# Router products on the scaled residual, with root and shift applied to the logits, in a one-core hybrid transformer layer

## The reference, cut to what matters

```python
def _layer(x, c, ...):
    mod = (silu(c) @ w_ada + b_ada)          # sh1, sc1, gt1, sh2, sc2, gt2 per sequence
    ...
    x = x + gt1 * mix                         # mix = merged @ w_out
    h = _rms_norm(x, norm_ffn_w) * (1 + sc2) + sh2
    x = x + gt2 * _hier_moe(h, lp)

def _hier_moe(h, lp):
    g_logits = t @ w_group_router + b_group_router      # 4 groups
    g_sel = argmax(g_logits)                            # and its softmax probability
    e_logits = t @ w_expert_router + b_expert_router    # 32 experts, 8 of the group kept
    top_p, top_i = top_k(softmax(e_logits), 2)
    comb = p_group * top_p / sum(top_p)
    out = sum over the 2 experts of comb * (silu(t@gate) * (t@up)) @ down
```

## Time and profile before

| | us |
|---|---|
| median of 3 runs | 838.47 |
| lowest, highest | 837.27, 840.47 |
| the profiled execution, its own time | 839.85 |
| its span in the trace | 838.1 |
| TensorE busy | 728.8 (87%) |
| weight loads busy | 529.4 (63%) |
| VectorE, ScalarE, POOL busy | 264.0, 195.1, 97.5 |
| mean granted TensorE clock, of full | 0.942 |

### The profile page before, as it was taken

How to read it: one execution, slowest core, us unless ns; L and a number is a source line. 1 busy time by engine, 2 the same in 40 slices (tenths; PEclk the granted TensorE clock), 3 DMA queues, 4 the chain that set the end, 5 groups by cost and what they waited for, 6 DMA issues and landing times.

```text
span 838.1 us, 19950 instructions
## 1 busy us (share of the span) xinstructions
PE 728.8 (87%) x8393; PEld 529.4 (63%) x8394; DVE 264.0 (32%) x737; ACT 195.1 (23%) x500; POOL 97.5 (12%) x229
## 2 busy tenths in 40 slices
PE   2779999999988975998988999973998989999985
PEld 1567777787766654776766777733655656656554
DVE  0145412430134350666683112144111111111122
ACT  1221113112731322122223200051111112121225
POOL 7000000001011222100000000001212221222200
PEclk9869999999999996999998999985899999999996
DMA  7835579999444954651002706875899999999901
GB/s 264 228 103 201 201 245 327 327 327 334 121 112 122 260 148 103 200 179 26 1 2 74 266 0 268 334 300 204 313 413 411 414 413 411 415 412 414 385 15 56
DMA packets 108728, 195.88 MB, mean 234 GB/s; under 512 B 9964, under 2 KB 71097, under 8 KB 100488
## 3 DMA queue, kind: packets, MB, share of 16 engines
q1 hardware_dynamic: 106760, 189.94, 63.1%
q0 software_dynamic: 1920, 5.25, 1.7%
HBM read 185.40 MB, written 9.77 MB: 233 GB/s over the span
## 4 chain that ended last, share of the span: by engine, by line
PE 81%; DVE 6%; DMA 4%; issue 4%; ACT 3%; SPq 1%; POOL 0%; ACTq 0%; DVEq 0%; POOLq 0%
PE ps L1142 17%; PE ps L533 10%; PE ps L1212 7%; PE ps L506 5%; PE ps L546 5%; PE ps L430 4%; PE ps L451 4%; PE ps L1084 4%; PE ps L509 3%; PE ps L434 2%; PE ps L496 2%; DMA arena<-in_w_ada 1%; SPq L811 1%; PE ps L540 1%; DVE arena L1894 1%
## 5 line engine op out<-in xcount | busy, mean ns | idle before, releaser
L1142 PE MATMUL ps<-arena 128*128 128x288 f32 x576 | 144.8, 411 | 0.0
L1142 PEld LDWEIGHTS ps<-arena 128*128 128x128 f32 x576 | 109.3, 192 | 31.2 <-issue 1.0
L533 PE MATMUL ps<-arena 128*32 128x128 f32 x2432 | 86.7, 278 | 15.3 <-issue 12.8
L533 PEld LDWEIGHTS ps<-arena 128*32 128x32 f32 x2432 | 69.3, 111 | 39.4 <-issue 38.2
L1212 PE MATMUL ps<-arena 128*128 128x288 f32 x256 | 76.2, 427 | 14.2 <-DMA arena<-in_w_in 10.3
L1212 PEld LDWEIGHTS ps<-arena 128*128 128x128 f32 x256 | 45.3, 194 | 30.1 <-DMA arena<-in_w_in 10.6
L506 PE MATMUL ps<-level,arena 32*128 32x256 f32 x624 | 44.8, 401 | 0.5 <-DVE arena L775 0.5
L546 PE MATMUL ps<-arena,hact 128*32 128x256 f32 x608 | 40.7, 385 | 0.0
L770 DVE TENSOR_TENSOR h_row<-h_row,ps 128x64 f32<-128x64 f32 x38 | 8.4, 221 | 96.6 <-ACT h_row L628 96.6
L404 POOL DMA_INDIRECT arena<-h_rows,idx_now x38 | 37.6, 988 | 9.5 <-issue 9.5
L1084 PE MATMUL ps<-arena,cT 128*32 128x128 f32 x1024 | 33.8, 292 | 4.6 <-DMA arena<-in_w_ada 4.6
(11 more groups left out here) (432 smaller groups left out, 983.0 us busy)
## 6 DMA issues: line engine op xcount, KB each, us to landing
arena<-in_w_exp_gate SPq DMA_DIRECT2D x32, 1024.0 KB
arena<-in_w_exp_up SPq DMA_DIRECT2D x32, 1024.0 KB
arena<-in_w_exp_down SPq DMA_DIRECT2D x32, 1024.0 KB
arena<-in_w_ada SPq DMA_DIRECT2D x12, 2048.0 KB, 10.2
arena<-in_w_in SPq DMA_DIRECT2D x18, 1024.0 KB, 5.9
arena<-in_w_ada_final SPq DMA_DIRECT2D x4, 2048.0 KB, 14.9
arena<-in_w_in SPq DMA_DIRECT2D x16, 512.0 KB, 4.7
arena<-in_state_ssm_rec SPq DMA_DIRECT2D x8, 512.0 KB, 6.0
```

Source lines behind the costliest of these rows:

```text
L533: l = mm(ps[CW * q:CW * (q + 1), 5, 0:P].rearrange("p (g f) -> p g f", g=2), xwin[:, at:at + CW], gate_up[:, :, k, f:f + HF], start=(k == ...
L1142: l = mm(ps[:, 2 + 2 * sl + m, 0:TOK], w_ring[sl][:, k, m * P:(m + 1) * P], HN[:, k, :], start=(k == 0), stop=(k == KT - 1))
```

## The change

The router's 8 products move into the output projection. ScalarE copies each prompt tile of xT times the scale into H2 right after squaring it (squares go to a buffer of their own, `sq2`), VectorE does the samples; TensorE then does tile k's router product behind its mean-square product (`logits`). The shift's part of the logits, shift @ w_rt, is 8 small products ahead of the projection (9 sequences by 36), to which VectorE adds the bias (`b_seq`). When the root is there, VectorE multiplies the 36 rows of logits by it, and TensorE transposes them and adds `seq_row` times `b_seq` (6 small products). The norm of H2 itself (times root, plus shift) is done by POOL in 8 + 1 instructions and by ScalarE in 8, beside the routing. The combining weights (`r_m`) are computed after the indices, and the second 24 slot products wait for them. In the loop the samples' part of PT is a block matrix of 128 columns, and one product takes the place of four. Place 6 of the ring loads its down weights first, and gate and up after the tables are done with.

```diff
+        q = ex_at + 2 * EXW + 3 * D
         r_n, q = carve(q, 4, E)
         r_c, q = carve(q, E)
         r_w, q = carve(q, 2, 6)
-        GE, q = carve(q, 6, NWIN + 1)
...
-        A6, q = carve(q, 6, NWIN)
+        GE, _ = carve(q, 6, NWIN + 1)
+        r_q, q = carve(q, E, 8)
+        A6, q = carve(q + 62, 6, NWIN)
...
-        PT, iota = late[:, 0:TOK], late[:, TOK:2 * TOK]
...
+        PTW = SEQ + 4 * SMP
+        PT, iota = late[:, 0:PTW], late[:, PTW:2 * PTW]
...
             wgu, wd = ex[6]
+            load(wd, wd_[:, 6], "ex_ld6")
+            e.wait_ge(S("count_mm"), 3)
+            e.wait_ge(S("tab"), 1)
             load(wgu[:, 0:KT, :], wg_[:, 6], "ex_ld6")
             load(wgu[:, KT:2 * KT, :], wu_[:, 6], "ex_ld6")
-            e.wait_ge(S("count_mm"), 3)
-            e.wait_ge(S("tab"), 1)
-            load(wd, wd_[:, 6], "ex_ld6")
...
-            e.wait_ge(S("x2"), KT)
-            link(g.iota(iota, pattern=[[1, TOK]], base=0, channel_multiplier=0, allow_small_or_imprecise_dtypes=True))
+            e.wait_ge(S("gate_mm"), NGATE)
+            e.wait_ge(S("merged"), KT)
+            link(g.memset(seq_row, 1.0))
...
+            g.memset(lg_row[:, TOK:], 0.0).then_inc(S("iota"), 1)
...
             e.wait_ge(S("stored"), 16 * rec_stores[0])
             g.memset(y_row, 0.0).then_inc(S("y_row"), 1)
             g.memset(PT, 0.0).then_inc(S("pt"), 1)
+            e.wait_ge(S("root"), 2)
+            e.wait_ge(S("rt_mm"), 2)
+            for k in range(KT):
+                g.tensor_tensor(out=H2[:, k, :], in0=H2[:, k, :], in1=rstd[:], op=ALU.mult).then_inc(S("h2"), 1)
+            e.wait_ge(S("h2"), KT)
+            s = H2[:, :, SEQ:TOK].rearrange("p k (b t) -> p k b t", t=NT)
+            g.tensor_tensor(out=s, in0=s, in1=modT[:, SHIFT2:SHIFT2 + KT, 1:NC].unsqueeze(3).broadcast_to([P, KT, NB, NT]),
+                            op=ALU.add).then_inc(S("h2"), 1)
...
-                l = mm(ps[:, bank, 0:TOK], ones[:, :], (H2 if n == 2 else sq3)[:, k, :], start=(k == 0), stop=(k == KT - 1))
+                l = mm(ps[:, bank, 0:TOK], ones[:, :], (sq2 if n == 2 else sq3)[:, k, :], start=(k == 0), stop=(k == KT - 1))
...
+
+            for k in range(KT):
+                l = mm(ps[0:NC, 2, 0:EG + E], modT[:, SHIFT2 + k, :], w_rt[:, k, :], start=(k == 0), stop=(k == KT - 1))
+            l.then_inc(S("rt_mm"), 1)
+
+            def logits(k):
+
+                e.wait_ge(S("x_scaled"), KT + k + 1)
+                e.wait_ge(S("x_mod"), KT + k + 1)
+                l = mm(ps[0:EG + E, 1, 0:TOK], w_rt[:, k, :], H2[:, k, :], start=(k == 0), stop=(k == KT - 1))
+                if k == KT - 1:
+                    l.then_inc(S("rt_mm"), 1)
 
             for m in range(KT):
                 if m >= 2:
                     e.wait_ge(S("x2"), m - 1)
...
 
             mean_square(2, KT - 2)
+            logits(KT - 2)
             mean_square(2, KT - 1)
-
+            logits(KT - 1)
+
+            e.wait_ge(S("lg_row"), 2)
+            e.wait_ge(S("iota"), 1)
+            for t in range(3):
+                cols = slice(t * P, (t + 1) * P)
+                mm(ps[:, 5, t * 36:(t + 1) * 36], lg_row[:, cols], ident[0:EG + E, 0:EG + E], start=True, stop=False)
+                l = mm(ps[:, 5, t * 36:(t + 1) * 36], seq_row[:, cols], b_seq, start=False, stop=True)
+            l.then_inc(S("rt_mm"), 1)
             e.wait_ge(S("y_row"), 1)
             for m in (1, 2, 3, 4, 0):
                 n = 4 * P if m < 4 else 2 * P
@@ -462,11 +511,8 @@
                 l = mm(ps[:, m, 0:n], y_row[0:SMP, 0:P], xT[0:SMP, :, :].rearrange("p k n -> p (k n)")[:, 0:n], start=True, stop=False)
             l.then_inc(S("comb_mm"), 1)
...
-            e.wait_ge(S("h2"), 1)
-            e.wait_ge(S("x_mod"), 2 * KT)
-            for k in range(KT):
-                l = mm(ps[0:EG + E, 5, 0:TOK], w_rt[:, k, :], H2[:, k, :], start=(k == 0), stop=(k == KT - 1))
-            l.then_inc(S("rt_mm"), 1)
+            e.wait_ge(S("h2"), KT + 1)
+            e.wait_ge(S("x_mod"), 3 * KT)
...
-                if t == 0:
-                    e.wait_ge(S("lg_row"), 1)
-                    for u, (o_, p_) in enumerate(TILES):
-                        l = tr(ps[0:p_, 5, u * 36:(u + 1) * 36], lg_row[:, o_:o_ + p_], ident[0:EG + E, 0:EG + E])
-                    l.then_inc(S("rt_mm"), 1)
...
-                for m in range(4):
-                    r = slice(CW * m, CW * (m + 1))
-                    l = mm(ps[r, 4, 0:2 * P], PT[r, SEQ:TOK], y_row[r, :], start=False, stop=last)
+                l = mm(ps[:, 4, 0:2 * P], PT[:, SEQ:PTW], y_row[:, :], start=False, stop=last)
                 l.then_inc(S("comb_mm"), 1)
...
-                act(H2[:, k, :], xT[:, k, :], ACT.Square).then_inc(S("sq"), 1)
+                act(sq2[:, k, :], xT[:, k, :], ACT.Square).then_inc(S("sq"), 1)
+                act(H2[:, k, 0:SEQ], xT[:, k, 0:SEQ], ACT.Copy, scale=scl[:, k, 0:1]).then_inc(S("x_mod"), 1)
             e.wait_ge(S("ms_mm"), 2)
             inverse_root(rstd[:], ps[:, 0, 0:TOK], D, "root")
-            prompt_modulated(H2, SHIFT2, 2)
+            for k in range(KT):
+                e.wait_ge(S("h2"), k + 1)
+                act(H2[:, k, 0:SEQ], H2[:, k, 0:SEQ], ACT.Identity, bias=modT[:, SHIFT2 + k, 0:1]).then_inc(S("x_mod"), 1)
...
+            norm_scale(colB[:, B_FFN:B_FFN + KT], SCALE2)
+            e.wait_ge(S("rt_mm"), 1)
+            tt(b_seq, ps[0:NC, 2, 0:EG + E], b_rt[0:NC, :], ALU.add).then_inc(S("lg_row"), 1)
             for m in range(KT):
                 e.wait_ge(S("wo_mm"), m + 1)
                 gated_add(m, ps[:, 4 + m % 2, :], GATE1, "x2")
-            e.wait_ge(S("x2"), KT)
-            norm_scale(colB[:, B_FFN:B_FFN + KT], SCALE2)
+                e.wait_ge(S("x2"), m + 1)
+                tt(H2[:, m, SEQ:TOK].rearrange("p (b t) -> p b t", t=NT), xT[:, m, SEQ:TOK].rearrange("p (b t) -> p b t", t=NT),
+                   scl[:, m, 1:NC].unsqueeze(2).broadcast_to([P, NB, NT]), ALU.mult).then_inc(S("x_scaled"), 1)
             e.wait_ge(S("root"), 2)
-            modulated(H2)
-            samples_modulated(H2, SHIFT2, 2)
-            e.nop().then_inc(S("h2"), 1)
-
-
-            e.wait_ge(S("rt_mm"), 1)
-            v.tensor_copy(lg_row, ps[0:EG + E, 5, 0:TOK]).then_inc(S("lg_row"), 1)
             e.wait_ge(S("rt_mm"), 2)
-            e.wait_ge(S("iota"), 1)
-            for t, (o, p) in enumerate(TILES):
-                l = tt(LG[0:p, t, :], ps[0:p, 5, t * 36:(t + 1) * 36], b_rt[0:p, :], ALU.add)
-            link(l)
+            tt(lg_row[:, 0:TOK], ps[0:EG + E, 1, 0:TOK], rstd[0:EG + E, :], ALU.mult).then_inc(S("lg_row"), 1)
+            e.wait_ge(S("rt_mm"), 3)
+            e.wait_ge(S("iota"), 2)
+            link(v.tensor_copy(LG, ps[:, 5, 0:108].rearrange("p (t x) -> p t x", t=3)))
...
-            e.wait_ge(S("h2t_mm"), 6)
             link(tt(r_eq, r_o1, r_o2, ALU.add))
             e.nop().then_inc(S("routed"), 1)
-
-            e.wait_ge(S("r_exp"), 1)
-            link(v.tensor_reduce(out=r_m[:, 3, :], in_=r_g2, op=ALU.add, axis=AX.X))
-            link(stt(r_m[:, 3, :], r_m[:, 6, :], 1.0, r_m[:, 3, :], ALU.add, ALU.mult))
-            link(v.reciprocal(r_m[:, 4, :], r_m[:, 3, :]))
-            link(tt(r_m[:, 5, :], r_m[:, 4, :], r_m[:, 6, :], ALU.mult))
 
...
-            tt(AV[:, 1], A6, r_m[:, 4:6, :].rearrange("p c t -> p (c t)").unsqueeze(2).broadcast_to([P, 6, NWIN]),
-               ALU.mult).then_inc(S("placed"), 1)
...
             ts(idx[:], ps[:, 6, 0:NWIN], 4.0, quarter, ALU.mult, ALU.add).then_inc(S("idx"), 1)
+            e.wait_ge(S("r_exp"), 1)
+            link(v.tensor_reduce(out=r_m[:, 3, :], in_=r_g2, op=ALU.add, axis=AX.X))
+            link(stt(r_m[:, 3, :], r_m[:, 6, :], 1.0, r_m[:, 3, :], ALU.add, ALU.mult))
+            link(v.reciprocal(r_m[:, 4, :], r_m[:, 3, :]))
+            link(tt(r_m[:, 5, :], r_m[:, 4, :], r_m[:, 6, :], ALU.mult))
+            tt(A6, A6, r_m[:, 4:6, :].rearrange("p c t -> p (c t)").unsqueeze(2).broadcast_to([P, 6, NWIN]),
+               ALU.mult).then_inc(S("placed"), 1)
...
-                ts(PT, iota[:, 0:TOK], slot_tab[:, 0, bass.ds(c, 1)], slot_tab[:, 1, bass.ds(c, 1)], ALU.is_equal,
+                ts(PT, iota, slot_tab[:, 0, bass.ds(c, 1)], slot_tab[:, 1, bass.ds(c, 1)], ALU.is_equal,
                    ALU.mult).then_inc(S("pt"), 1)
```

45 lines of the change are left out of this document (30 added, 15 removed).

## The result

| us | before | after |
|---|---|---|
| median (20 runs of each) | 838.25 | 841.67 |
| lowest, highest | 835.23, 842.70 | 837.47, 844.13 |
| span of the profiled execution | 838.1 | 839.4 |

The ratio is 1.0038 with an interval of 1.0026 to 1.0050. The change makes the kernel some 3 us slower where 7.3 us of gain were forecast. The time lies above the predicted range of 827.0 to 836.5.

What follows compares the result with a forecast made beforehand. The prediction took TensorE's work, and behind the projection an uncovered chain through TensorE and VectorE, as the bound. Its terms, +2.9 + 1.0 - 7.4 - 3.8 = -7.3 us, gave 831.2 against a median of 838.47; range 827.0 to 836.5.

Steps and rivals of the forecast that it cites:

- signs of being wrong: Two observations named ahead as refuting the forecast: counts later than 566 us, or a loop window of unchanged length.
- The projection: Output projection: six of eight added router products fall between tiles on the path, 0.486 us each, +2.9 us.
- a narrower weight does not shorten the stream of columns: Output projection: a router product with 36 weight columns still takes 0.486 us, as its 288 streamed columns set the price.
- The shift products: Ahead of the projection: eight small products wait for `merged` on the path, priced between 0.6 and 1.6 us, taken as +1.0.
- Behind the projection: From the projection's last product to the end of the counts: 19.7 us instead of 27.15, so -7.4.
- The shared access: SBUF use behind the projection: POOL's norm delays VectorE's routing about 4 us; POOL waiting in turn adds 0.9.
- Rival 1: Behind the projection: shared SBUF access hurts more, counts start at 17.4 instead of 15.6; 833.6 us in all, chance 0.15.
- The loop: Expert loop: one samples' product for four saves 0.10 us a window, times 38 gives -3.8 us.
- in the projection they hide under products of 0.24 each: Samples' product in the loop: its two 128-column weight loads, 0.190 us each, taken as hidden, as in the projection.
- Rival 3: Expert loop: both wide weight loads stand in the open in each window, +9.5 instead of -3.8; 844.5 us, chance 0.07.
- Rival 2: Counts behind the projection: the clock holds at 2.4 GHz, so they take 2.0 us; 829.2 us in all, chance 0.12.
- Rival 4: Expert loop: no gain, the wait only moves to the hidden row's copy or the weights; 835.0 us, chance 0.12.

Runs made afterwards that it cites:

- the best kernel: The kernel after with H2's norm on VectorE, two banks opened before transposes, three after counts, 128-column router weight, samples' single product behind transposes: 825.51 us, ratio 0.9849.

## Why the prediction was wrong

By the stages the forecast missed by 10 us: 5.9 in the loop, 2.4 behind the projection, 2.0 in it. Two of its own signs of being wrong came true, the counts began at 567.76 and a window did not get shorter (5.83 before, 5.89 after).

**The projection** (forecast +2.9, measured +4.9). The step that failed is "a narrower weight does not shorten the stream of columns", taken to mean that width has no other effect. The stream was 0.486 as priced, and 0.13 + 0.20 us of exposed loads came with each of six tiles. The wide weight took 1.92 us of them away, which shows this reason.

**The shift products** (+1.0, measured +0.6). The bound from the slot products, 0.074 each, was the better one.

**Behind the projection** (-7.4, measured -5.0). The structure came out as worked out: H2 was complete 10.0 us behind the projection (forecast 10.6), the routing 15.7 (forecast 15.4), and the transposes decided. But three sizes on TensorE were off. The six small products of the logits took 2.1 us instead of 0.6, so the opening started 5.77 behind the projection instead of 4.4; 0.10 apiece was read from transposes of one record each, while these have two records and take 0.34 to 0.41. The opening took 6.37 instead of 5.36. So it ended 12.1 behind the projection, after H2; the transposes then started 1.5 later than forecast. They ran at half clock, 6.34 instead of 5.0. The counts gave back 0.4. These are +1.5, +1.3 and -0.4, the missing 2.4. How it splits between the three depends on when the clock came back, as the other profiles of this stage show; the sum hardly does. That the opening held the transposes is shown by the run with the opening behind the counts.

**The shared access.** The delay of VectorE was forecast about right: its small steps stretched to 0.74 while POOL worked. The 0.9 for POOL waiting in turn was wrong: POOL's eight took 6.05, 0.756 apiece, and kept that pace before VectorE's chain had begun as well as during it. Here the trace doesn't bear out the Trainium skill's page SBUF — State Buffer, section "Who interferes with whom", as far as it says that issue order decides who blocks: VectorE waited, POOL didn't. Rival 1 was no part of the loss.

**The loop** (-3.8, measured +2.1). This step decided the sign. The step that failed is "in the projection they hide under products of 0.24 each", taken from loads between products of one shape. The samples' product follows row-tiled products of 32x128, and its first load did not start under them. The place takes 0.63 and not 0.46. Rival 3 had this mechanism and the point from which it decides (+0.09 a window), but with both loads in the open on top of 0.43; only about one was, 0.20. It came out at +0.055 a window, a small form of that rival. The other terms came to +0.7 together, so the kernel got slower; with the forecast's -3.8 it would have been 3 us faster. Its chance of 0.07 was too low, as the argument against it rested on rows of another neighbourhood. The rows held a warning: L509's place took 0.56 for four products on pieces of the array, where a single stream of 256 columns is 0.43.

**Rival 2** didn't occur in this profile: the counts ran at 1.2 GHz. In three other profiles of the same stage, and in the best kernel, they ran mostly or wholly at 2.4, and in the same stage this gained nothing, as the opening had then run longer at the low clock. The argument against the rival, that the opening let the clock fall, isn't borne out (last section). **Rival 4** named the copy of the hidden row as a wait that might come; it was there all along, 0.19 a window on the loads, and a product moved in front of down was worth more than any other edit of the loop. How much of that the wait itself explains is open.

**The range.** Its ends don't follow from the terms: rival 2 with the loop at its best gives 831.2 - 2.1 - 1.1 = 828.0, and rival 4 with H2 late by 1.8 gives 836.8. The measured time lies beyond either.

Not settled: how far a narrower load must differ for it not to be hidden (only 128x36 and 32x128 beside 128x128 were varied), why down, gate and up get shorter with a product ahead of down, and whether that needs the wait for the copy at all.

## What to carry to other kernels

Price an inserted product with the change of tile shape on both sides of it, not by its columns: ask which neighbour's load is hidden now, and take the price from a row where a shape follows another. Padding a narrow weight to the neighbours' width can be free and faster. In a tight window look for a product that waits for a copy just made (here down, 0.19 us on its load), and try independent products ahead of it before making those products shorter; here that was worth 0.28 to 0.39 us of a window of 5.9.

## What the runs showed of the hardware

- A weight load of another tile shape than the one before it stood in the open: 0.13 us for 128x36 behind 128x128, 0.20 for 128x128 behind 128x36 or behind row-tiled 32x128. Behind products of the same shape the wide router weight and the samples' weight in the new place cost nothing beyond the stream of columns (0.48 and 0.43), although the first loads more columns.
- Beside POOL's tensor-tensors on 288 columns, four small two-input instructions of VectorE in a row took 0.74 us each, as long as one of POOL's, where they take 0.10 to 0.17 without POOL; a reduction took 0.17 beside POOL as well, and POOL's own pace of 0.756 us was the same before and beside them.
- The clock falls without the opening of the sums. In the kernel before with the late opening TensorE had nothing to do from 545.7 to 550.7, and the clock fell within that; windows of TensorE alone:

```profile
545.72:548.72 3.00, 0.00 (x0) 1.00 0.80 333
548.72:549.72 1.00, 0.00 (x0) 0.85 1.01 426
549.72:550.72 1.00, 0.00 (x0) 0.50 1.04 442
```

In four profiles of variants of the kernel after (the four products back, the late opening, and the single and the four products behind the transposes) it also fell before the opening had begun, 4.5 to 4.6 us behind the projection's end, during the small products of the logits. In the kernel after it fell 7.1 us behind it, with TensorE idle from 552.0 to 553.0 and then at work without a gap. The forecast had put the fall to the opening.
